# Mixing prompt and sample apart, each beside the other's expert rows

## The reference, cut to what matters

```
for l in range(2):
    mod = silu(c) @ w_mod[l] + b_mod[l]                # for prompt and for sample
    h = layer_norm(x) * (1 + sc_a) + sh_a
    z = h @ w_in[l]
    t = merge(attention(z), retention(z), rwkv7(z)) @ w_out[l]   # token mixing
    x = layer_norm(ALPHA * x + gt_a * t)
    h = layer_norm(x) * (1 + sc_f) + sh_f
    scores = (h @ wq) against 2 x 128 keys, 8 heads; the 16 best pairs of each head
    act = gelu(u[eidx] . h) * softmax(best)            # 128 experts for each token
    x = layer_norm(ALPHA * x + gt_f * sum(act * v[eidx]))
```

## Time and profile before

| | us |
|---|---|
| median of three runs | 4149.53 |
| profiled execution, its own time | 4141.36 |
| its span | 4139.5 |
| TensorE busy | 3200.9 |
| VectorE busy | 2070.3 |
| GpSimd busy | 1552.6 |
| ScalarE busy | 719.0 |

### The profile page before, as it was taken

One profiled execution on the slowest core, in us unless ns is written; L12 is line 12 of the kernel. 1 busy time (PEld: TensorE's weight loads), 2 busy tenths in 40 slices (PEclk: granted clock), 3 DMA queues, 4 the chain that ended last, 5 costly groups with the idle time before them and its releaser, 6 DMA issues.

```text
span 4139.5 us, 48070 instructions
## 1 busy us (share of the span) xinstructions
PE 3200.9 (77%) x18671; PEld 1650.5 (40%) x18671; DVE 2070.3 (50%) x4872; ACT 719.0 (17%) x1702; POOL 1552.6 (38%) x1702
## 2 busy tenths in 40 slices
PE   5998498996577677777869975989856776776777
PEld 1555387554122222222325554865432222222222
DVE  4135644036765656754151356430467756657441
ACT  0112321002111111111101132210011111111111
POOL 1200000002677677767511000000027776776774
PEclk8999699998899999999979987999979999999999
DMA  8421000225999899989873210002249998998997
GB/s 319 92 82 59 14 6 13 102 81 190 366 409 403 341 410 407 406 344 406 311 257 99 72 60 2 6 33 102 103 159 382 404 410 342 409 406 349 401 409 255
DMA packets 299120, 974.80 MB, mean 235 GB/s; under 512 B 28842, under 2 KB 31088, under 8 KB 298768
## 3 DMA queue, kind: packets, MB, share of 16 engines
q0 software_dynamic: 228608, 822.50, 52.1%
q1 hardware_dynamic: 70288, 149.23, 10.0%
HBM read 967.95 MB, written 3.67 MB: 235 GB/s over the span
## 4 chain that ended last, share of the span: by engine, by line
PE 41%; DMA 27%; POOL 12%; DVE 11%; issue 7%; ACT 2%; DVEq 0%; SPq 0%; POOLq 0%; ACTq 0%
DMA arena<-in_peer_v,arena 18%; PE ps L496 10%; PE ps L1817 6%; POOL arena L1715 6%; PE ps L1404 6%; POOL arena L1704 6%; DMA arena<-in_peer_u,arena 5%; PE ps L1416 3%; DMA ring<-in_w_mod 3%; PE ps L1430 2%; DVE arena L1751 2%; PE ps L1150 1%; PE ps L1142 1%; PE ps L1107 1%; PE ps L1153 1%
## 5 line engine op out<-in xcount | busy, mean ns | idle before, releaser
L1817 PE MATMUL ps<-arena 128*128 128x512 f32 x3072 | 1501.7, 614 | 616.2 <-DMA arena<-in_peer_v,arena 531.7
L1751 DVE CUSTOM_DVE_ANT_0 arena<-arena,ps 128x1024 f32<-128x1024 f32 x768 | 937.1, 1221 | 754.9 <-DMA arena<-in_peer_u,arena 650.5
L1817 PEld LDWEIGHTS ps<-arena 128*128 128x128 f32 x3072 | 528.7, 191 | 1585.0 <-ACT arena L1789 801.3
L1715 POOL DMA_INDIRECT arena<-in_peer_v,arena x768 | 725.2, 944 | 394.1 <-PE ps L1817 271.2
L1704 POOL DMA_INDIRECT arena<-in_peer_u,arena x768 | 729.1, 949 | 378.9 <-issue 204.1
L1789 ACT ACTIVATE arena<-const,arena 128x128 f32<-128x128 f32 x768 | 296.0, 398 | 1256.6 <-PE ps L1817 1256.6
L496 PE MATMUL ps<-hT,ring 128*128 128x384 f32 x1248 | 423.5, 495 | 8.9 <-ACT hT L460 8.9
L496 PEld LDWEIGHTS ps<-hT,ring 128*128 128x128 f32 x1248 | 235.6, 192 | 172.4 <-issue 15.1
L1404 PE MATMUL ps<-hT,ring 128*128 128x384 f32 x768 | 248.0, 486 | 0.0
L1404 PEld LDWEIGHTS ps<-hT,ring 128*128 128x128 f32 x768 | 145.8, 190 | 102.0 <-issue 0.7
L1521 POOL DMA_DIRECT2D arena<-in_peer_keys x2 | 2.3, 1172 | 472.6 <-issue 472.6
(11 more groups left out here) (321 smaller groups left out, 3523.4 us busy)
## 6 DMA issues: line engine op xcount, KB each, us to landing
ring<-in_w_in SPq DMA_DIRECT2D x30, 2048.0 KB, 7.9
ring<-in_w_mod SPq DMA_DIRECT2D x24, 2048.0 KB, 9.1
ring<-in_w_br SPq DMA_DIRECT2D x6, 2048.0 KB, 7.9
arena<-in_peer_u,arena POOLq DMA_INDIRECT x768, 7.8
arena<-in_peer_v,arena POOLq DMA_INDIRECT x768, 7.7
ring<-in_w_out SPq DMA_DIRECT2D x4, 2048.0 KB, 8.4
ring<-in_peer_wq SPq DMA_DIRECT2D x4, 2048.0 KB, 7.8
arena<-in_na_rpb POOLq DMA_DIRECT2D x64, 64.0 KB, 5.4
```

Source lines behind the costliest of these rows:

```text
L1715: pool.indirect_dma_start(vrow[m % NBUF], None, v_rows, bass.IndirectOffsetOnAxis(ap=row_no[t][:, k:k + 1], axis=0))\
L1751: nc.vector.tensor_tensor_reduce(product[n % 2].rearrange("p (c d) -> p c d", c=2), urow[n % NBUF].rearrange("p (c d) -> p c d", c=2), h_b ...
L1817: ins = nc.tensor.matmul(row_acc(t)[c][:, :], diag[n % 4], vrow[n % NBUF][:, 512 * c:512 * (c + 1)], start=(k == 0), stop=(k == P - 1))
```

## The change

The token sets are taken apart. The order of the program becomes: modulation of layer 0; mix of the prompt, layer 0; mix of the sample, layer 0; ten chunks of modulation of layer 1; mix of the prompt, layer 1; two chunks of modulation; mix of the sample, layer 1; rows of the sample, layer 1. A mix is stages 2 to 7 over one tile (prompt, T = 128) or two (sample, T = 256). The weight chunks of a mix, 23, are therefore read twice a layer.

The expert rows of a mix are now a generator on each engine, cut into visits (`yield`): 162 for the prompt's 128 rows, 298 for the sample's 256. They ride in the next mix: `pump(engine, stage, i)` stands at fixed places of each engine's mixing program and advances the generator to the visit that `RIDE` gives for that place. Only the last mix's rows have nothing above them. Every engine stays in order: what is pumped stands between two pieces of mixing.

```diff
+UNIT_BY = {"p": [0, 8, 20], "s": [0, 16, 40, 70, 100]}
+ROWBUF = {"p": 3, "s": 4}
+MIXES = [("p", 0), ("s", 0), ("p", 1), ("s", 1)]
+RIDE = {"s": {"proj": (0, 62, 39), "ret": (62, 82, 2), "prep": (82, 94, 3), "scan": (94, 130, 24), "merge": (130, 170, 60)},
+        "p": {"proj": (0, 112, 39), "ret": (112, 134, 2), "prep": (134, 150, 3), "scan": (150, 190, 12),
+              "merge": (190, 304, 60)}}
...
+            riding = {"rows": None, "at": 0, "end": 0, "tag": None}
+            def advance(v):
+                while riding["at"] < min(v, riding["end"]):
+                    next(riding["rows"])
+                    riding["at"] += 1
+            def pump(who, stage, i):
+                if who == key and riding["rows"] is not None:
+                    first, last, n = RIDE[riding["tag"]][stage]
+                    advance(first + (last - first) * (i + 1) // n)
+            for tag, l in MIXES:
+                mod(eng, l, FIRST[tag])
+                riding["tag"] = tag
+                run = mix(tag, l, pump)[key]
+                run(*(args if key in ("act", "dve") else (eng,)))
+                advance(riding["end"])
+                rows = experts(tag, l)
+                make = rows[key]
+                riding.update(rows=make(eng, link) if key == "dve" else make(eng), at=0, end=rows["end"])
+            advance(riding["end"])
...
+                for z in range(NZ):
+                    pump("pe", "proj", z)
+                    c, j = divmod(z, 4)
...
+                        ins = nc.tensor.matmul(z_bank(z), w[:, k, P * j:P * (j + 1)], hT[:, k, tokens],
+                                               start=(k == 0), stop=(k == KT - 1))
...
+                for j in range(LEVELS):
+                    if j:
+                        pump("pe", "scan", LEVELS * s + j)
...
+            def pool_mix(pool):
+                pool_decays(pool)
+                pool_rwkv_in(pool)
+                pool_na(pool)
+                pump("pool", "proj", NZ - 1)
+                pool_na_out(pool)
...
+            def meet(m):
+                return m + LAG + GAP * (m // P)
+            END = meet(NROW - 1) + 3
...
+            def pe_rows(pe):
+                n = 0
+                for v in range(END):
+                    while n < NROW and meet(n) <= v:
+                        t, k = divmod(n, P)
+                        if k == 0 and t:
+                            pe.wait_ge(sem("peer_res"), at("peer_res", 2 * t))
+                        pe.wait_ge(sem("diag"), at("diag", n + 1))
+                        row_here(pe, "v", n)
+                        for c in range(2):
+                            ins = nc.tensor.matmul(row_acc[c][:, :], diag[n % 4], vrow[n % NB][:, 512 * c:512 * (c + 1)],
+                                                   start=(k == 0), stop=(k == P - 1))
+                        ins.then_inc(sem("v_used"), 1)
+                        n += 1
+                    yield
...
-                nc.vector.tensor_tensor_reduce(product[n % 2].rearrange("p (c d) -> p c d", c=2),
-                                               urow[n % NBUF].rearrange("p (c d) -> p c d", c=2), h_bank, 1.0, 0.0, ALU.mult, ALU.add,
-                                               row_dot[t][:, k:k + 1]).then_inc(sem("u_used"), 1)
...
+                        row = urow[v % NB].rearrange("p (k d) -> p k d", k=KT)
+                        nc.vector.tensor_tensor_reduce(row, row, hT[:, :, P * (t0 + t):P * (t0 + t + 1)], 1.0, 0.0,
+                                                       ALU.mult, ALU.add, row_dot[t][:, k:k + 1]).then_inc(sem("u_used"), 1)
```

More of the change, by code:

```diff
@@ L250, in build @@
[L250 to L255, removed]
@@ L346, in finish @@
                 ins.then_inc(sem("mod_spread"), 1)
-            for c in range(12):
-                w = chunk_here(pe, l, c)
+            for c in chunks:
+                w = chunk_here(pe, "mod", l, c)
                 if c >= 2:
@@ new lines, in dve_proj @@
+            def dve_proj(dve, link):
+                for z in range(NZ):
+                    pump("dve", "proj", z)
+                    if z % 2:
+                        dve.wait_ge(sem("proj"), at("proj", z + 1))
+                        nc.vector.tensor_copy(ZT[:, z, :], z_bank(z)).then_inc(sem("z_dve"), 1)
+                    if sample and z in BIAS_AT:
+                        dve_bias(dve, BIAS_AT.index(z))
+                    if z >= NA_TILES:
+                        dve_na_step(dve, link, z - NA_TILES)
+                    if z > R_RW:
+                        dve_shift(dve, link, z - 1)
+                dve_shift(dve, link, NZ - 1)
@@ L1104, in pe_rwkv_step, with level, later, heads @@
+            def level(s, j, d):
+                return 2 * (LEVELS * s + j) + d + 1
+            def later(s, j, d):
+                return 2 * ((LEVELS - 1) * s + j - 1) + d + 1
+            def heads(fn, dirs=(0, 1)):
+                for d in dirs:
                     for z in range(4):
@@ L1578, in top16 @@
[L1578 to L1595 removed]
+                pe.wait_ge(sem("merged"), at("merged", 8))
@@ new lines, in pe_merge @@
+                pe.wait_ge(sem("gate_act"), at("gate_act", 24))
+                w_half = [None, None]
+                for n in range(2 * nt):
+                    pump("pe", "merge", 36 + 2 * n)
+                    t, c = divmod(n, 2)
+                    if t == 0:
+                        w_half[c] = chunk_here(pe, tag, l, 19 + c)
+                    for k in range(KT):
+                        ins = nc.tensor.matmul(ps[OUT_BANK[n]][:, :], merged[:, k, P * t:P * (t + 1)], w_half[c][:, k, :],
+                                               start=(k == 0), stop=(k == KT - 1))
+                    ins.then_inc(sem("out_mm"), 1)
@@ L1821, in pe_peer @@
[L1821 to L1832 removed]
+                    for i in range(n):
+                        ins = nc.vector.max_index(idxs[i][:, 8 * half:8 * half + 8], vals[i][:, 8 * half:8 * half + 8], values[i])
+                        if i < n - 1:
+                            yield
```

2831 lines of the change are left out of this document (1486 added, 1345 removed).

## The result

The changed kernel takes **4387.14 us** (median of 4 runs, 4385.74 to 4415.0) against 4148.85 for the kernel before (four runs, 4147.34 to 4154.65): 5.9% slower, ratio 1.0588 with a 95% interval of 1.0544 to 1.0631. I had forecast 4070, with a range of 3860 to 4310. The profiled execution took 4385.7 us, its span is 4383.9; by my stages I had summed 4060, so 324 us have to be found.

What follows compares the result with a forecast made beforehand. TensorE (898 us of mixing) and the DMA engines (1076 us of expert rows) were taken to bound each layer in turn. 1417 us of lone rows leave, 1087 return riding, splitting adds 232 and modulation 19: 4070 us, range 3860 to 4310.

Steps and rivals of the forecast that it cites:

- rival B: Riding rows: the engines' order couples them, bringing a row back to 2.62 us; 256 us more, 4326 us; chance 0.25.
- read port: Dot product reading two SBUF operands: priced at nothing; as a rival, fetches wait, 0.48 us a row, 4316 us, chance 0.07.
- Ride of the prompt's rows in the sample's mixes: Sample mix carrying the prompt's 128 rows, both layers: the rows add 263 us, making each mix 893 us.
- 19 us lost: Start of the sample's mix: VectorE's selection and GpSimd's loads come first, TensorE has three tiles meanwhile; 19 us lost.
- 34 us that I gave to coupling: Sample's mixes: engines waiting for one another at pumps, ScalarE's table switches and closing norm; 34 us, bounds 0 and 100.
- Ride of the sample's rows in the prompt's mix: Prompt mix of layer 1 with the sample's 256 rows: fetches nearly bound it; 561 us of ride, 945 us in all.
- Mixes alone: Split mixing without rows: prompt 384 us, sample 630, together 1014 against 898, so 116 us more in each layer.
- costs nothing by itself: Second reading of the mixing weights, 46 MB a layer: lies under matmuls and costs nothing by itself.
- Lone rows: The sample's 256 rows of layer 1, alone at the end: ramp 71 us plus 664 us, 735 us.
- Modulation: Layer 1's modulation parameters, fetched only after the selection before has ended: ten chunks 75 us, two chunks later 20 us.
- what a riding row costs: Expert rows carried in the next mix: 512 rows at 2.12 us each, 1087 us.
- The probe I had named: Ride's stage time minus stage time alone, over rows: above 2.3 us or below 1.8 a row, the prediction is wrong.

Runs made afterwards that it cites:

- zonly: The kernel both, with ScalarE alone emptying the first twelve projection tiles, of which VectorE emptied every second: 4292.98 us, ratio 1.0335 to the kernel before.
- ahead2: The changed kernel, with ScalarE making each row's diagonal two visits ahead of TensorE instead of one: 4390.23 us, ratio 1.0579 to the kernel before.
- noride: The changed kernel with split mixing, but each mix's expert rows run alone before the next mix, nothing riding: 4810.25 us, ratio 1.159 to the kernel before.
- sbufh: The kernel before, with h copied once a token tile from PSUM to SBUF for the dot product, its product tiles kept: 4244.59 us, ratio 1.0231.
- both: The changed kernel with VectorE's selections due later and only a few visits in retention and preparation: 4295.04 us, ratio 1.0354 to the kernel before.
- psumh: The changed kernel, with h of the last 256 rows, which run alone, kept in four PSUM banks: 4365.81 us, ratio 1.052 to the kernel before.
- biassp: zonly with the first selection dealt out over six visits, and SyncE instead of GpSimd issuing the 32 bias loads: 4284.21 us, ratio 1.0321.

## Why the prediction was wrong

**The mechanism that fits best is rival B's**, the engines' order coupling the ride: it gave 4326 us at 2.62 us a riding row, and the row costs 2.64. That the two figures agree is luck: 2.62 was the price of a lone row, borrowed, while the 2.64 is a mean of 2.54 in the sample's mixes and 2.75 in the prompt's, and holds the read port too. What the experiments show of the coupling are the bursts (83 us) and the first selection (19 us); two other guesses of where it sits, VectorE's copies (zonly) and ScalarE's diagonals (ahead2), gained nothing. Term by term, the 324 us, each ride as the stage's time in the change less its time in noride:

- *Ride of the prompt's rows in the sample's mixes* (263 each; measured 325 and 326, by noride). Projection 111 where I had 75: "19 us lost" at the start was too little, because I took one selection ahead of VectorE's copies and not the two behind it, with the first row 6 us late. Retention 86 where I had 40: I let a burst go at the fetches' 2.57 us; with three buffers the issue waits for a dot, the landing for the issue and TensorE for the landing. Scan 65 where I had 43, or 1.8 a row: 0.37 us a level was there to fill. Preparation 16 (15), gates to output 49 (56). Without the 34 us that I gave to coupling my terms were 229; so the coupling, the port and my misreadings together came to 96, near the bound of 100 that I had set for it and far from the 34 that I summed.
- *Ride of the sample's rows in the prompt's mix* (561; measured 703). Projection 290 (231): for 111 us VectorE has 97 us of selection, dots and copies; afterwards the DMA share is 0.94 at 346 GB/s, not the 407 by which I counted rows and weights. That 407 was a steady stretch; the earlier trace rows has 383 over its 1005 us. Retention and preparation 115 (78), scan 72 (61), the rest 232 (191). The norm takes 5 us less than in noride. My scan term also counted 40 rows where 32 meet TensorE: the accumulator changes over to the second tile there, and eight visits carry no row. So my 561 us were for 264 rows.
- *Mixes alone* (2028; measured 2070). The sample's are 673 and 678 (630), 33 us of it in the projection; the prompt's 355 and 364 (384), in the change 351. The 128-column matmuls go at 0.118 us each, not 0.160. The chain of waits of the prompt's gates in the changed kernel says what that is:

```profile
322.33 7.58 PE ps L1552 x64
329.92 7.80 DMA ring<-in_w_in
337.76 7.42 PE ps L1552 x64
```

  64 matmuls in 7.6 us alternate in the chain with the landing of a 2.1 MB chunk in 7.8: at 128 columns the two-slot ring is as slow as TensorE, so the second reading of the weights, which "costs nothing by itself" in the prediction, is at its limit (TensorE is still busy 66.1 of the 68.5 us of these stages). The four matmuls of the earlier trace rows were no measure of long series.
- *Lone rows* (735; measured 752) and the *read port*, which I priced "at nothing": I had read one row, in which the fetch begins 0.03 us after the VectorE operation. A fetch that begins so early goes ahead: in sbufh all nine that begin 0.02 to 0.04 us after a dot product's start take 0.94 us. From 0.06 us on they wait. The trace of the kernel before had that case as well, an operation of the same line with 1024 columns, and I missed it; below it is the change:

```profile
1106.27 1.22 DVE L1666 TENSOR_TENSOR arena<-arena,const 128x1024 f32<-128x1024 f32 x1
1106.71 1.61 POOL L1704 DMA_INDIRECT arena<-in_peer_u,arena  x1 [0.30 <-issue]
```

```profile
1046.17 1.22 DVE L2017 CUSTOM_DVE_ANT_1 arena<-arena,hT 128x1024 f32<-128x1024 f32 x1
1046.52 1.68 POOL L1952 DMA_INDIRECT arena<-in_peer_u,arena  x1 [3.02 <-DVE arena L2017]
1048.50 0.94 POOL L1952 DMA_INDIRECT arena<-in_peer_v,arena  x1 [0.30 <-issue]
```

  The fetch at 1046.52 us begins with 0.87 us of the dot product to go and takes 0.74 longer than the next, which meets none. The prediction cites the Trainium skill, "SBUF — State Buffer", section "Who interferes with whom", which says that the two contend and calls the shared ports an exclusive lock. I held my one row against it, and the traces agree with the page: the fetch that comes second waits the dot product out. "Fully blocks", the prediction's other words, stands on the page for another kind of VectorE instruction, and the traces show it for this one too. The mean rises by 0.10 us only because most fetches meet none.
- *Modulation*, 73 (75), was right; TensorE's busy sum, +100 (+130), came out 30 us lower than forecast.

So the sum fails by 62 + 63 + 142 = 267 us on the rides, 42 on the mixes and 17 on the lone rows, 326 against the 324 to be found; modulation and the end about cancel. The step that failed is **"what a riding row costs"**: I priced each engine's own work, read an idle 1.0 us into each level of the scan, and gave the order 34 us. The probe I had named (stage time with the ride minus without, over rows) shows 2.64 where the sum has 2.12, over the 2.3 at which I said the prediction falls. Part of TensorE's longer busy time is its clock (0.898 against 0.939); what that is worth was not measured apart.

Moving visits out of the bursts, later selections and dealing out the first one win back 113 us together (4387 to 4274), which leaves the kernel 3% slower than the one before. No version that was run beats 4149. A ride's price would have to be some 2.15 us at the split's measured cost: 4149 less the mixes alone (2070), both modulations and ends (some 223) and the last rows (752) is 1104 us for 512 rows. In the kernel both, the sample's first mix came to 2.25; the prompt's stayed near 2.6. What bounds a row there at the last, fetches at 346 to 384 GB/s or VectorE, was not taken apart.

## What to carry to other kernels

Where work is woven into another stage at fixed points, price the order first: at each point take the slowest engine's whole queue (selection, copies and dots together), and a burst at issue + landing + use, not at the bandwidth, when the buffers are fewer than the burst. Idle time of a stage is of use only in the pieces in which it comes: a level with 0.37 us free takes no 1.85 us row. Time that a chain of waits gives to another engine isn't idle time of this one: ask the window how busy it was. One row of a trace can't rule out contention: look at every instruction of the kind, sorted by where it begins in the other. And a split into two programs has fixed costs that a ride must earn before it gains; here 274 us of mixing and a ramp for each block.

## What the runs showed of the hardware

- A VectorE dot product with two SBUF operands holds up a GpSimd indirect fetch that begins within it until it ends: in sbufh 588 such fetches take 1.21 us on average, the other 948 take 0.95. The mean goes from 947 to 1047 ns, and the kernel before gets 2.3% slower; in psumh, with one operand in PSUM for the last rows, their fetches are back at 0.94 and 0.95 us. A TENSOR_TENSOR of two SBUF operands does the same (1.61 us at 1106.71 us of the kernel before). Dot products that begin within a fetch aren't lengthened: 678 of them in sbufh take 1.23 us.
- Rows alone move at 407 GB/s in a steady stretch and at 383 with a DMA share of 0.98 over 1005 us. With weight chunks between them the change moves 346 GB/s at a share of 0.94 (1640 to 1915.6 us) and 384 at 1.00 (2228 to 2380 us).
- 32 bias loads of 64 KB fill the DMA engines: from 461 to 476 us they are busy 1.00 of the time at 94 GB/s, and a row's fetch behind them lands in 11.2 us instead of 5.25. In biassp a weight chunk behind them lands in 21.1 us, where the change's chain has 7.8 in the prompt's gates.
- TensorE's granted clock is lower in stretches with many gaps: 0.67 in the first 111 us of the prompt's second projection (busy 41 us), 0.56 in the preparation of the kernel before (busy 20 of 66.5 us), 1.00 in gates and branches. Such figures are means over a stretch, between its two levels of 1.2 and 2.4 GHz. Over the span the mean fell from 0.939 to 0.898; a row's matmul (L2072) took 641 ns on average where L1817 took 614.
